# Two transformer models in one kernel, one core: the order of each engine's work where two stages meet

## Time and profile before

| | |
|---|---|
| median of 3 runs | 1416.14 us (1414.89 to 1416.19) |
| profiled execution, first to last instruction | 1408.7 us |
| PE busy in it | 1335.9 us, 95% |
| DVE / ACT / POOL busy | 944.4 / 643.6 / 149.4 us |
| mean DMA rate | 216 GB/s |

### The profile page before, as it was taken

One profiled execution on the slowest core, in us unless ns is written; L12 is line 12 of the kernel. 1 busy time (PEld: TensorE's weight loads), 2 busy tenths in 40 slices (PEclk: granted clock), 3 DMA queues, 4 the chain that ended last, 5 costly groups with the idle time before them and its releaser, 6 DMA issues.

```text
span 1408.7 us, 17661 instructions
## 1 busy us (share of the span) xinstructions
PE 1335.9 (95%) x6207; PEld 1082.7 (77%) x6207; DVE 944.4 (67%) x1122; ACT 643.6 (46%) x845; POOL 149.4 (11%) x215
## 2 busy tenths in 40 slices
PE   5999999799999999999998899999899999999997
PEld 2678887688888788887786678887687777788885
DVE  4788887878887788886566375465586566464442
ACT  2443344544444533345466543345555654543341
POOL 3100001201010100100240100001017000000000
PEclk9999999999999999999999899999999999999999
DMA  9999885599895699864543385555346434465540
GB/s 329 335 350 329 304 308 199 208 303 333 305 315 175 237 313 309 309 220 133 159 145 97 118 292 175 189 179 170 115 138 229 155 134 134 137 205 194 193 154 30
DMA packets 179910, 304.82 MB, mean 216 GB/s; under 512 B 8516, under 2 KB 122580, under 8 KB 179592
## 3 DMA queue, kind: packets, MB, share of 16 engines
q1 hardware_dynamic: 159272, 224.62, 47.6%
q0 software_dynamic: 20576, 79.37, 16.1%
HBM read 302.91 MB, written 1.05 MB: 216 GB/s over the span
## 4 chain that ended last, share of the span: by engine, by line
PE 43%; ACT 4%; DVE 3%; issue 1%; POOL 1%; POOLq 0%; DVEq 0%; ACTq 0%
PE ps L496 13%; PE ps L498 13%; PE ps L497 13%; ACT whi L1270 2%; DVE wlo L1858 1%; PE ps L939 1%; ACT ps L1343 1%; PE ps L577 0%; PE ps L919 0%; ACT xn L1372 0%; DVE xres L2144 0%; DVE xn L2141 0%; DVE ntlo L2179 0%; PE ps L650 0%; ACT xn L1352 0%
## 5 line engine op out<-in xcount | busy, mean ns | idle before, releaser
L1858 DVE TENSOR_TENSOR wlo<-raw,whi 128x2048 fp32r<-128x2048 f32 x212 | 481.7, 2295 | 88.7 <-ACT whi L1270 86.0
L496 PE MATMUL ps<-whi,nthi 128*128 128x512 f32 (+1 forms) x1264 | 509.7, 403 | 9.0 <-DVE ntlo L2179 6.6
L498 PE MATMUL ps<-whi,ntlo 128*128 128x512 f32 (+1 forms) x1264 | 496.3, 393 | 0.0
L497 PE MATMUL ps<-wlo,nthi 128*128 128x512 f32 (+1 forms) x1264 | 495.4, 392 | 0.0
L1270 ACT ACTIVATE whi<-raw 128x2048 fp32r<-128x2048 f32 x212 | 397.4, 1909 | 75.7 <-DMA raw<-in_ffn_w_gu 30.1
L496 PEld LDWEIGHTS ps<-whi,nthi 128*128 128x128 f32 x1264 | 240.7, 190 | 58.1 <-issue 7.9
L498 PEld LDWEIGHTS ps<-whi,ntlo 128*128 128x128 f32 x1264 | 240.1, 190 | 51.9
L497 PEld LDWEIGHTS ps<-wlo,nthi 128*128 128x128 f32 x1264 | 241.1, 191 | 46.0
L1899 DVE SCALAR_TENSOR_TENSOR arena<-arena,cact 128x512 f32<-128x512 f32 x238 | 178.8, 751 | 10.3 <-DMA arena<-in_mod_w 2.6
L496 PE MATMUL ps<-whi,hthi 128*128 128x512 f32 x440 | 173.8, 395 | 5.9 <-DVE htlo L1949 4.5
L498 PE MATMUL ps<-whi,htlo 128*128 128x512 f32 x440 | 172.1, 391 | 0.0
(11 more groups left out here) (256 smaller groups left out, 855.8 us busy)
## 6 DMA issues: line engine op xcount, KB each, us to landing
raw<-in_ffn_w_gu SPq DMA_DIRECT2D x176, 512.0 KB, 5.2
arena<-in_mod_w POOLq DMA_DIRECT2D x72, 1024.0 KB, 6.7
raw<-in_ffn_w_down SPq DMA_DIRECT2D x88, 512.0 KB, 5.5
raw<-in_w_in SPq DMA_DIRECT2D x44, 512.0 KB, 4.6
raw<-in_w_gate_up SPq DMA_DIRECT2D x44, 512.0 KB, 4.9
raw<-in_diff_w_qkv SPq DMA_DIRECT2D x24, 512.0 KB, 4.6
raw<-in_w_down SPq DMA_DIRECT2D x22, 512.0 KB, 6.0
raw<-in_diff_w_o SPq DMA_DIRECT2D x8, 512.0 KB, 4.1
```

What stands on the lines that cost most here:

```text
L496: pe.matmul(o, hi, wh, start=start, stop=False)
L497: pe.matmul(o, hi, wl, start=False, stop=False)
L498: return pe.matmul(o, lo, wh, start=False, stop=stop)
L1858: v.tensor_tensor(wlo[:, s * PIECE:(s + 1) * PIECE], raw[:, r * PIECE:(r + 1) * PIECE], hi, ALU.subtract).then_inc(w_lo, 1)
```

## The change

No arithmetic changes: the same instructions run on each engine in another order.

- **PE, head of ffn1 to ffn4.** `turn_join` of the second tokens moves from behind block A to the middle of block B, behind `turn_one(0, A)`.
- **ACT, join, behind an ffn (in front of ffn2 and of attention).** The split of `splits[1]` moves behind `second_half`, `one_hi(0, 1)` (the copy of the last inner columns) and `x_hi` of the first tokens.
- **ACT, all joins with a split behind `scaled_rows(1)`.** That last split moves into the next head, behind `gated_half(0, A)`; in an ffn head `one_hi(0, 0)` follows it, and `second_half(1)` and `x_hi(1)` come behind.
- **DVE, ffn head.** `first_half(1)` moves behind the split and `one_lo(0, 0)`.
- The join in front of the second mix keeps its order. DVE's `if final` is nested below `if tail`; the one final join has both.

```diff
 # PE, ffn_head
                 mm.then_inc(filled[A], 1)
-                turn_join((1,))
                 o = bank(B)
                 for h in range(2):
                     w1.append(views())
                     mm = block_half(o, 0, h, w1[h])
                     if h == 0:
                         turn_one(0, A)
+                        turn_join((1,))
...
 # ACT, join
-                split(splits[1])
-                if tail is not None and squared == 2:
+                if tail is not None and squared == 1:
+                    second_half(0, j, g_cols, shift)
                     one_hi(0, 1)
-                second_half(0, j, g_cols, shift)
-                if tail is not None and squared == 1:
-                    one_hi(0, 1)
-                x_hi(0, j)
+                    x_hi(0, j)
+                    split(splits[1])
+                else:
+                    split(splits[1])
+                    if tail is not None and squared == 2:
+                        one_hi(0, 1)
+                    second_half(0, j, g_cols, shift)
+                    x_hi(0, j)
                 split(splits[2])
                 for _ in range(squared):
                     squares(1)
-                last = min(splits[3], 1)
-                split(splits[3] - last)
+                split(splits[3])
                 scaled_rows(1, squared)
-                split(last)
                 return j
 # ACT, ffn_head
                 gated_half(0, full(A))
+                split(1)
+                one_hi(0, 0)
                 second_half(1, j, g_cols, shift)
                 x_hi(1, j)
-                one_hi(0, 0)
                 gated_half(1, full(B))
 # ACT, blocks_head (first=1 for attention, 0 for the second mix)
                 keep(0, 0, full(A))
+                split(first)
                 second_half(1, j, *g_cols)
 # ACT, the calls
-            j = join(*norm, (0, 0, 0, 2))
+            j = join(*norm, (0, 0, 0, 1))
             at = ffn(1, j, norm, True)
-            j = join(*norm, (2, 1, 1, 1), tail=at)
+            j = join(*norm, (2, 1, 1, 0), tail=at)
             at = ffn(2, j, norm, True)
-            j = join(*norm, (2, 1, 1, 1), tail=at)
+            j = join(*norm, (2, 1, 1, 0), tail=at)
             diff_attention(j, *norm)
-            j = join(*norm, (2, 0, 1, 1))
+            j = join(*norm, (2, 0, 1, 0))
             at = ffn(3, j, norm, True)
...
-            j = join(*norm, (2, 0, 1, 1))
+            j = join(*norm, (2, 0, 1, 0))
             at = ffn(4, j, norm, False)
 # DVE, ffn_head
                 product(0, A)
+                split(1)
+                one_lo(0, 0)
                 first_half(1, j, g_cols, shift)
-                split(1)
-                one_lo(0, 0)
                 x_lo(1)
```

More of the change, by code:

```diff
@@ L1468, in first_head, with blocks_head @@
                 split(4)
-            def blocks_head(j, g_cols, p, keep, ahead=1):
+            def blocks_head(j, g_cols, p, keep, first=1, ahead=1):
                 keep(0, 0, full(A))
+                split(first)
                 second_half(1, j, *g_cols)
@@ L1696, in others @@
                     nc.scalar.activation(dst, ps[:, 2 + (b + 1) % 2, :], func).then_inc(blk_read[1], 1)
-                blocks_head(j, (g_cols, None), START["in"], keep, 2)
+                blocks_head(j, (g_cols, None), START["in"], keep, 0, 2)
                 n.next(M)
@@ L1955, in ffn_head @@
                 product(0, A)
-                first_half(1, j, g_cols, shift)
                 split(1)
                 one_lo(0, 0)
+                first_half(1, j, g_cols, shift)
                 x_lo(1)
@@ L2213, in join @@
                     product(1, B)
-                if final:
-                    one_lo(0, 1)
+                    if final:
+                        one_lo(0, 1)
                 first_half(0, j, g_cols, shift)
```

## The result

| | before | changed |
|---|---|---|
| first comparison, median (5 runs each) | 1414.89 us | 1402.22 us (1401.07 to 1406.67) |
| ratio to before, 95% interval | | 0.9926 [0.9904, 0.9949] |
| again, on another occasion (28 and 5 runs) | 1414.15 us (1408.58 to 1417.05) | 1403.08 us, 0.9926 [0.9908, 0.9943] |
| span of the profiled execution | 1408.7 us | 1402.5 us |

By the ratio, which is what later comparisons use too, the changed kernel is 0.74% faster, some 10.5 us (0.0074 x 1414.15), where 7.6 were predicted; the medians themselves lie 12.7 and 11.1 us apart. The direction was right. The size was not, and neither was the base: the shown median of 1416.14 came from three runs, and 28 give 1414.15 (17 on a third occasion give 1415.23).

A forecast was written before the change was run, and what follows sets the result against it. PE, busy 1335.9 of 1408.7 us, was the bound, so only its waits could shrink: 3.3 (ffn2) + 1.9 (attention) + 1.6 (ffn3) + 0.7 (ffn4) + 0.1 (ffn1) = 7.6 us; 1416.1 - 7.6 = 1408.5 us, range 1405.5 to 1413.0.

The forecast's parts named there:

- Copy ahead of the split: Joins before ffn2 and attention: PE's waits for `htlo` go whole, 1.89 and 1.48 us.
- `joined` out from behind the split: Joins before ffn2 and attention: DVE's weight split runs earlier, so the second tokens' chain gains 0.4 us on PE.
- The turning in ffn2 hidden: ffn2's head: PE turns the second tokens' rows without a wait, 1.17 + 0.24 = 1.4 us won.
- the second tokens' rows in time: ffn heads: last `ntlo` comes before PE needs it; slack 2 us in ffn2, about 1.3 in ffn1 and ffn3.
- The drain: ffn3 and ffn4: about 1.38 us beside the table load, not counted; with it 1.4 and 0.7 us less won, 1410.6 us.
- the upper bound of 9.9 us: Gain if all these waits in ffn1 to ffn4 and attention went: 9.9 us, giving 1406.3 us.
- The 7.4 us "outside the span": Whole kernel: the median of the runs lies 7.4 us above the profiled span of 1408.7 us, taken as fixed.
- ffn3's wait: ffn3's head, at `turn_one`: a new wait of 1.0 us replaces the old ones; 1.6 us won.
- The returned wait: Heads: silu chain or second tokens' late rows cost what the turning gave; gain 3.4 to 4.5 us, some 1412; 20%.
- The time was not given back: Stages after the heads: weights or DVE set the pace and take the gain back; 1414 to 1416 us; 11%.
- The clock rival: Four ffn heads: ten transposes in a row halve the clock, 3.4 us lost each, 13.6 in all; 1422 us; 5%.
- the first rival: Heads: the turning's part comes back as another wait; gain 3.4 to 4.5 us, some 1412; 20%.

The follow-up runs named there:

- late_2: Changed kernel plus two scratch copies on ACT ahead of the first tokens' `second_half`, before ffn2 and attention; 1405.07 us, one execution.
- heads_only: Changed kernel with the reordered branch of ACT's join (inner columns' copy ahead of the weight split) put back; ratio to before 0.9960.
- tail_only: Kernel before with only ACT's join reordered: last inner columns' copy ahead of the weight split, before ffn2 and attention; ratio to before 0.9971.
- pe_only: Kernel before with only PE's move: second tokens' rows turned in the middle of block B, ACT and DVE in old order; ratio to before 1.0017.
- orders_only: Changed kernel without PE's move: the second tokens' turning stays behind block A; ratio to before 0.9941.
- late_1: Changed kernel plus one scratch copy on ACT ahead of the first tokens' `second_half`, before ffn2 and attention; 1409.0 us, one execution.
- gate_early: Changed kernel with ACT making the last group's silu ahead of the scaled rows in the join before the second mix; ratio to before 0.9889.

## Why the prediction was right and wrong, point by point

- **The mechanism** was right in each place. Copy ahead of the split: both waits gone, `htlo` at 461.24 where the working gives 461.3 when shifted by this trace's 3.67 us. `joined` out from behind the split: 0.4 us, seen as 1.17 to 0.78 at attention's turning. The turning in ffn2 hidden, `turn_one` not late, the second tokens' rows in time: the last `ntlo` at 478.50, PE's need of it at 479.8, so 1.3 us of slack where 2 were predicted. Between the table load and the activation there are 0.02 us (802.47 + 1.28, then 803.77). The drain that the Trainium skill, "ScalarE: Activation LUTs", section "What ACT_TABLE_LOAD costs", puts beside the load does not show in this trace, and the prediction rightly did not price it.
- **The step that failed: the price of a wait.** The sum counted a removed wait at the idle that the trace prints. Predicted and found in the stretches: ffn2 3.3 and 4.07 (two waits), attention 1.9 and 2.17 (one), ffn4 0.7 and 1.19 (two), ffn3 1.6 and 1.88 (three for one). `late_2` measures it by itself, 0.30 us a wait, and with it ffn2 comes to 3.9, attention to 2.2, ffn4 to 1.3. ffn3, two waits fewer, would come to 2.2, more than its 1.88; counted with the wait as it was at the same clock (`heads_only`), 1.43 us of idle went and 1.89 us were won, 0.23 us a wait. In all the stretches are 1.8 us above the sum; the ratio is 2.9 above it. The same omission lay in the upper bound of 9.9 us, and so in the low end of the range.
- **The second one: the base.** The 1416.1 us of three runs were 2.0 us above the median of 28. The 7.4 us "outside the span" were a sign of this that I read over: they are 1.7. The 6.3 us between 1408.5 and 1402.2 are thus 2.0 of base, 2.9 of gain, of which the stretches place 1.8, and 1.5 by which the median of the first five runs lies below what the ratio gives (1403.7), for which I have no cause but the spread of single executions.
- **ffn3's wait** was predicted at 1.0 and is 2.07. PE had 3.4 us less of low clock in front of it in this trace than in the first (6.8 us), and came to `turn_one` earlier, while the chain of scaled rows came at the same distance from the first turning (12.3 us). With 6.8 us of low clock the wait is 1.24 (`heads_only`). The size of the wait follows the clock in front of it, and the gain does not: what ends the wait is ACT's and DVE's chain, so a PE that arrives earlier waits longer. `tail_only` shows this for the old order, with no low stretch in that join, 2.24 us of waiting at the turning instead of 1.22, and ffn3's stretch as before (-0.01).
- **The rivals.** The returned wait is what `pe_only` shows: it comes if the orders on ACT and DVE are left. The time was not given back as that rival had it, through weights or DVE: behind the heads the stretches agree within 0.1 us, but for the clock, in attention's first block and in the join before the second mix (1.0 to 1.1 us lost). The clock rival did not occur: the ten transposes stand in a row in four heads, and neither of the changed kernel's traces has a low stretch behind them in ffn2, ffn3 or ffn4. The remark on transposes in the Trainium skill, "TensorE: Matmul & The Clock Gate", section "Part 4: PE-mode transpose", would by the prediction's reading have had the clock fall there; these traces do not bear that out for ten transposes (1.3 us). Only in `pe_only` did a low stretch begin during them, in ffn3 and behind a wait of 3.89 us; which of the two it followed is not separated.
- **A slip in the chances**: four fifths of the first rival's 0.20 are 0.16, not 0.18, so "faster" came to 0.80.
- **Open**: the measured 10.5 us against the 9.4 of the stretches, or the 8.1 to 9.1 of whole traces. The interval of the ratio, 8.1 to 13.0 us, holds them all. The rest may be chance, or rarer falls of the clock: time at the lower level, worked out from each execution's granted clock, averages 49.6 us in 28 executions of before (51.0 in 17 others) and 46.5 and 48.2 in twice five of the changed kernel. How often a wait of this join is followed by a fall is not measured.

## What to carry to other kernels

When an engine with a hand-written order is the bound, price each wait at its idle plus the restart behind it (0.2 to 0.4 us here), and look in front of it for work of another engine that nobody waits for yet: here a weight split that was itself waiting for its transfer. A move on the bound engine alone can lose: its new first wait must be freed on the other engines in the same change. And take the base from many executions, and check that the profiled one's time and its span are a pair.

## What the runs showed of the hardware that was not expected

A low stretch of 3.4 us stood right behind a wait of 2.11 us in `orders_only` and one of 2.24 in `heads_only`, but none stood behind waits of the same size in ffn3: 2.24 in `tail_only`, 2.11 in `late_1`, 2.12 in `gate_early`, 2.07 in the changed kernel.
```profile
803.73 1.27 PE L650 MATMUL ps<-ident,xn 128*128 128x128 f32 x8 [2.24 <-ACT xn L1372]
```
(That row is `tail_only`'s.) One and the same place differs between executions of the same program: in attention's first block PE waits 2.30 us at L909, and behind it the first trace of before has a low stretch (696.1 to 699.5, 1.6 us longer) and the second has none. In six of all 13 traces a low stretch begins around the end of this wait (from 0.4 us ahead of it to 1.1 us behind), and in five of the 13 within 1.4 us behind another one, of 2.19 us at L659 (1186.0 in the first trace of before), where each cost some 1.2 us. So waits of this size carry a chance of a fall and not a certainty, and single traces must be compared by stretch.
